# Block two of a two-block transformer layer on one core: where the head outputs are kept, gated and merged

## The chip, the cores and the metric

The kernel runs on one core of a Trainium2 chip. The metric is the device time of one execution in microseconds (us), the median of several runs. A profiled execution has its own time and its span, which runs from the first to the last instruction. Engines are named as in the profile: PE is TensorE (PEld its weight loads), ACT is ScalarE, DVE is VectorE, POOL is GpSimd, SP is SyncE; ACTq and SPq are the issues of DMAs by those engines.

## What is computed

The reference is two transformer blocks in a row on one sequence of 512 tokens by 1024 features, in float32. Block one (mLSTM heads, stick-breaking heads, an MLP) is untouched here. Block two, cut to what matters:

```python
h = rms_norm_2(x, norm_gain)
proj = h @ w_in                      # c_q, c_kv, ..., gate_a, gate_b, ..., m_a, m_b
# kind 0: 8 MLA heads of width 64 (causal softmax), kind 1: 8 DSA heads of width 64
#         (softmax over the top 128 keys that an indexer picks)
o_a = mla_attention(q_a, k_a, v_a) * silu(gate_a)        # 512 x 512
o_b = dsa_attention(q_b, k_b, v_b, ...) * silu(gate_b)   # 512 x 512
m = sigmoid([m_a, m_b] + b_merge)
y = m[0] * (o_a @ w_branch_mla) + m[1] * (o_b @ w_branch_dsa)
x = x + y @ w_out
```

`silu(g)` is `g * sigmoid(g)`, so an output is multiplied once by `g` and once by `sigmoid(g)`.

## The kernel before

Everything is one program with five instruction streams that meet at counting semaphores (`S[name]`). Activations stand transposed in SBUF, features on the 128 partitions and the 512 tokens along the free axis; `o_all[:, i]`, `g_all[:, i]` and `m_all[:, j]` are such tiles of 128x512. Weights come in groups `g` of 1024x512 from `wall`: SP loads a group in two halves into `w_raw`, ACT rounds a half to the short format (`split_hi`, L255), DVE makes the remainder (`split_lo`, L261). `project` (L288) then makes one 128x512 product tile in PSUM bank `proj[:, n % 2]` as three matmuls for each k tile (hi x hi, hi x lo, lo x hi). Before tile `n` PE waits for `tile_free >= n - 1`, so at most two tiles are unevicted; `tile_made` counts what PE made, `tile_free` what was evicted.

The end of block two has three stages.

1. **Head pairs B = 0 to 7** (0 to 3 are kind 0, 4 to 7 kind 1). In each pair PE does: turn q and k (L1379), gate tile 0, scores (L1386), gate tile 1, turn p (L1396), gate tile 2, p times v (L1404). The 24 gate tiles `T_L + 3 B + i` are `gate_a`, `gate_b` (8 tiles) and `m_a`, `m_b` (16 tiles); ACT evicts each to `gate_st` and stores it to DRAM (`gates_d`, L781 and L783). DVE does the masked maxima and the normalization, ACT the exponentials (L760), the eviction of p transposed (`head_pT`, L766) and of the pair's output (`head_out`, L773), which goes to `o_st` and from there to DRAM (`o_d`, L806). POOL stages q, k and v (L450, L451, L472). In loop form (`Fori`) two pairs are one iteration.
2. **Branch products, tiles T_BR + 0 to 15**, below T0 to T15: T0 to T7 multiply kind 0's gated outputs by `w_branch_mla` (group G_BR), T8 to T15 kind 1's by `w_branch_dsa` (G_BR + 1); a tile is 12 matmuls. PE's tile T0 waits for the four remainders of kind 0 (`oh_lo`), T8 for those of kind 1. DVE evicts each tile by multiplying it with its merge gate (L1208).
3. **Final product, T_FIN + 0 to 7**, 24 matmuls each, on the merged activations; DVE adds them to `x_fin` and SP stores the result.

Between stages 1 and 2 the outputs come back: POOL loads `o_all[:, 0:4]` and `g_all` in pair 5 (L481, L482), `o_all[:, 4:7]` and `m_all[:, 0:6]` after pair 7's staging (L489, L494), `o_all[:, 7:8]` when pair 7's output is stored (L496), then `m_all[:, 6:16]` (L499) and `x_fin` (L500). POOL multiplies `o_all` by `g_all` (L486 for tiles 0 to 3 in pair 6, L504 for 4 to 7). The function `gated(kind, ...)` stands in ACT's and in DVE's stream: ACT takes the sigmoid of `g_all` (L815), DVE multiplies (L1184), ACT rounds to `h_hi` (L818), DVE makes `h_lo` (L1190). In ACT's stream the order after pair 7 is `gated(0)`, sigmoids of merge gates 0 to 3 (`merge_gates`, L823), both halves of `split_hi(G_BR + 1)`, merge gates 4 and 5, `gated(1)`, merge gates 6 to 15. In DVE's stream it is `gated(0)`, then a loop over the 16 tiles, with `split_lo(G_BR + 1)` ahead of the evictions of T1 and T2 and kind 1's gating spread over T3 to T7; `split_lo(G_FIN)` stands ahead of T10 and T12. From T8 on POOL adds the two kinds (L508), ACT rounds the sum (`mg_hi`, L837) and DVE makes `mg_lo` (L1194).

## Time and profile before

| what | us |
|---|---|
| median of 3 runs | 1409.86 (1407.19 to 1410.21) |
| the profiled execution: its time | 1410.33 |
| the profiled execution: its span | 1408.6 |
| mean granted TensorE clock | 0.977 of full |
| PE busy / PEld busy | 1331.4 / 1066.5 |
| DVE / ACT / POOL busy | 701.6 / 638.7 / 124.8 |

What lies around the span of the profiled execution is 1.7 us. Engine times overlap, so they don't add up to the span; what sets the end is read from the chain of work that ended last, and what an engine's idle time is worth from the wait that ended it. Matmul records overlap their neighbours by some tenths of a microsecond, so the pace of PE is taken from start to start.

### The profile page before, as it was taken

Reading aid. Unit: us, or ns where it says so; the run is one execution under the profiler, and the core shown is the slowest. Engines: PE = TensorE matmul, PEld = TensorE weight load, DVE = VectorE, ACT = ScalarE, POOL = GpSimd, SP = SyncE. Lnnn points to the kernel's source line nnn. Section 1 sums busy time; section 2 is a strip of 40 time slices with the busy share of each in tenths; the row PEclk is TensorE's granted clock in tenths of the full one; section 3 lists DMA queues with packets and bytes.
Section 4 is the critical chain, followed back from the end, with each engine's and each line's share of the span. In section 5 each row is a group of like instructions: output and inputs, shape, how many; then the busy total and the mean of one; then the engine's idle time right before and its main releaser. Section 6 shows DMA issues by size and latency. Waiting matters only on the chain.

```text
span 1408.6 us, 16618 instructions
## 1 busy us (share of the span) xinstructions
PE 1331.4 (95%) x6008; PEld 1066.5 (76%) x6008; DVE 701.6 (50%) x1161; ACT 638.7 (45%) x927; POOL 124.8 (9%) x232
## 2 busy tenths in 40 slices
PE   4799999999999998999999999999878999999699
PEld 3677878777787776788888888878646777777577
DVE  5344443454444443452443424453798887443661
ACT  5455564555635561441332313353725454554540
POOL 1010100101000010000000000000112111140230
PEclk9899999999999999999999999999978999999899
DMA  5312122222222213123222322241111323535511
GB/s 204 105 64 89 53 89 76 84 67 67 97 67 93 67 63 140 69 94 116 89 89 92 111 95 89 94 170 69 60 60 55 118 97 102 205 102 188 209 60 60
DMA packets 26608, 138.05 MB, mean 98 GB/s; under 512 B 3400, under 2 KB 3464, under 8 KB 13520
## 3 DMA queue, kind: packets, MB, share of 16 engines
q1 hardware_dynamic: 15792, 109.06, 22.3%
q0 software_dynamic: 5168, 18.08, 3.9%
q10 hardware_dynamic: 5616, 10.49, 2.0%
q8 instruction: 19, 0.31, 0.1%
q14 instruction: 13, 0.11, 0.0%
HBM read 123.97 MB, written 12.60 MB: 97 GB/s over the span
## 4 chain that ended last, share of the span: by engine, by line
PE 89%; DVE 5%; ACT 3%; DMA 2%; issue 1%; ACTq 0%; POOL 0%; DVEq 0%; POOLq 0%
PE proj L288 72%; DMA x_res<-in_x 2%; PE pa L1288 2%; PE pm L1247 1%; PE pm L1295 1%; PE pm L1404 1%; PE pa L1254 1%; PE pa L1404 1%; PE pa L1247 1%; PE pa L1386 1%; PE pm L1386 1%; PE pa L1265 1%; PE pm L1396 1%; DVE rope L1034 1%; PE pm L1274 1%
## 5 line engine op out<-in xcount | busy, mean ns | idle before, releaser
L288 PE MATMUL proj<-h_hi,w_hi 128*128 128x512 f32 x1040 | 419.3, 403 | 17.7 <-DVE h_lo L1190 11.0
L288 PE MATMUL proj<-h_lo,w_hi 128*128 128x512 f32 x1040 | 407.7, 392 | 0.0
L288 PE MATMUL proj<-h_hi,w_lo 128*128 128x512 f32 x1040 | 407.6, 392 | 0.0
L261 DVE TENSOR_TENSOR w_lo<-w_raw,w_hi 128x2048 fp32r<-128x2048 f32 x102 | 234.3, 2309 | 172.6 <-ACT w_hi L255 170.0
L255 ACT ACTIVATE w_hi<-w_raw 128x2048 fp32r<-128x2048 f32 x102 | 193.4, 1911 | 159.0 <-PE proj L288 147.1
L288 PEld LDWEIGHTS proj<-h_hi,w_hi 128*128 128x128 f32 x1040 | 197.1, 189 | 65.2 <-issue 18.2
L288 PEld LDWEIGHTS proj<-h_hi,w_lo 128*128 128x128 f32 x1040 | 196.8, 189 | 42.3
L288 PEld LDWEIGHTS proj<-h_lo,w_hi 128*128 128x128 f32 x1040 | 197.3, 190 | 41.5 <-issue 2.9
L288 PE MATMUL proj<-w_hi,act_hi 128*128 128x512 f32 x256 | 99.6, 389 | 0.0
L288 PE MATMUL proj<-w_hi,act_lo 128*128 128x512 f32 x256 | 99.6, 389 | 0.0
L288 PE MATMUL proj<-w_lo,act_hi 128*128 128x512 f32 x256 | 99.6, 389 | 0.0
L999 DVE TENSOR_TENSOR x_res<-x_res,proj 128x512 f32<-128x512 f32 x32 | 21.9, 686 | 101.8 <-PE proj L288 101.8
L641 ACT ACTIVATE relu<-proj 128x512 f32<-128x512 f32 x32 | 19.2, 599 | 106.9 <-PE proj L288 106.9
L985 DVE TENSOR_TENSOR relu_sq<-relu 128x512 f32<-128x512 f32 x32 | 22.2, 694 | 76.3 <-ACT relu L641 76.3
L288 PEld LDWEIGHTS proj<-w_hi,act_hi 128*128 128x128 f32 x256 | 48.0, 188 | 10.1
L288 PEld LDWEIGHTS proj<-w_hi,act_lo 128*128 128x128 f32 x256 | 48.0, 188 | 10.0
L288 PEld LDWEIGHTS proj<-w_lo,act_hi 128*128 128x128 f32 x256 | 48.0, 188 | 9.9
L760 ACT ACTIVATE p_sb<-p_sb,mx 128x128 f32<-128x128 f32 (+1 forms) x64 | 35.1, 550 | 32.9 <-DVE mx L1133 32.9
L288 PE MATMUL proj<-w_hi,h_hi 128*128 128x512 f32 x96 | 38.0, 396 | 0.9 <-DVE h_lo L323 0.9
L288 PE MATMUL proj<-w_lo,h_hi 128*128 128x512 f32 x96 | 37.4, 390 | 0.0
L288 PE MATMUL proj<-w_hi,h_lo 128*128 128x512 f32 x96 | 37.4, 389 | 0.0
L422 POOL DMA_DIRECT2D x<-x_res x1 | 0.8, 769 | 402.1 <-DVE x_res L999 402.1
(354 smaller groups left out, 1865.3 us busy)
## 6 DMA issues: line engine op xcount, KB each, us to landing
w_raw<-in_wall SPq DMA_DIRECT2D x102, 1024.0 KB, 5.1
gates<-gate_st ACTq DMA_DIRECT2D x24, 256.0 KB, 2.0
m_all<-gates POOLq DMA_DIRECT2D x1, 2560.0 KB, 12.2
x_res<-in_x ACTq DMA_DIRECT2D x4, 512.0 KB, 11.7
bc<-gate_rows POOLq DMA_DIRECT2D x8, 256.0 KB, 3.4
x_res<-in_x POOLq DMA_DIRECT2D x1, 2048.0 KB, 11.7
x<-x_res POOLq DMA_DIRECT2D x1, 2048.0 KB, 7.1
heads_out<-o_st ACTq DMA_DIRECT2D x8, 256.0 KB, 2.0
```

The costliest lines, as they stand in the source:

```text
L255: nc.scalar.activation(w_hi[:, slot, 4 * half:4 * half + 4, :], w_raw[:, half], ACT.Copy)\
L261: nc.vector.tensor_tensor(w_lo[:, slot, 4 * half:4 * half + 4, :], w_raw[:, half], w_hi[:, slot, 4 * half:4 * half + 4, :], ALU.subtract)\
L288: mm = nc.tensor.matmul(proj[:, bank, :], lhsT, rhs, start=(k == 0 and q == 0), stop=(k == kts - 1 and q == 2))
L641: a.activation(relu[:, i % 2], proj[:, i % 2], ACT.Relu).then_inc(S["tile_free"], 1)
L760: a.activation(x, x, ACT.Exp, bias=mx[:, u, i:i + 1], accum_out=row_sum[:, u, i:i + 1])\
L985: v.tensor_tensor(relu_sq[:, i % 2], relu[:, i % 2], relu[:, i % 2], ALU.mult).then_inc(S["a_sq"], 1)
L999: v.tensor_tensor(xx, xx, proj[:, t % 2], ALU.add).then_inc(S["tile_free"], 1)
L1034: v.tensor_tensor(dst, xx, w, ALU.mult).then_inc(S["rope"], 1)
L1247: mm = t_.matmul(out_[:, TRI[i]:TRI[i] + SEQ - P * i], lhsT[0:rows, P * i:P * (i + 1)], rhs[0:rows, P * i:], start=True, stop=True)
L1288: mm = t_.matmul(pa[:, TRI[i] + P * (i2 - i):TRI[i] + SEQ - P * i], w[:, :], s_[:, TRI[i2]:TRI[i2] + SEQ - P * i2], start=(q == 0), stop=( ...
L1386: mm = t_.matmul(X[:, LOW[i]:LOW[i] + P * (i + 1)], qT[u][0:d, P * i:P * (i + 1)], kT[u][0:d, 0:P * (i + 1)], start=True, stop=True)
L1404: mm = t_.matmul(X[:, P * i:SEQ], v_st[u][:, i, :], pT[u][:, TRI[i]:TRI[i] + SEQ - P * i], start=(i == 0), stop=(i == TB - 1))
```

## The change

- `head_out` of pairs 4 to 7 writes straight into `o_all[:, B]` instead of `o_st`; the DRAM stores of these pairs and POOL's two loads of them (L489, L496) are gone. ACT's and DVE's loops over pairs 4 to 7 are written out.
- POOL loads `o_all[:, 0:4]` and `g_all` in pair 4 instead of pair 5. `m_all[:, 0:6]` waits for fewer gate stores, and the last load of merge gates is cut in two: `m_all[:, 6:10]` and `m_all[:, 10:16]`, after all gate stores and `pv0`; `x_fin` follows `o_sb1`.
- All eight products by `g_all` are on DVE (`times_g`): tiles 0 to 3 in pair 6, 4 to 7 after pair 7's DVE work. The eight merge sums are on DVE, right behind the eviction of T8 to T15.
- Kind 0's gating moves ahead of T0: in pair 7 ACT does the four sigmoids between gate tile 1 and `head_pT`, and the four roundings between `head_pT` and gate tile 2; DVE does the four products, `times_g(4)` to `times_g(6)`, and the four remainders.
- Rounded outputs stand in `og_hi` (over `g_all`) and `og_lo` (over `o_all`); the merged ones in `h_hi` and `h_lo`.
- ACT's order after pair 7 is: merge gates 0, 1; sigmoids of `g_all` 4 to 7; merge gates 2, 3; `split_hi(G_BR + 1)` twice; roundings 4 to 7; merge gates 4 to 15. DVE's: ahead of T1's eviction `split_lo` half 0 and products 4, 5; ahead of T2's `split_lo` half 1 and products 6, 7; remainders 4 to 7 ahead of T3 to T6.

```diff
@@ GpSimd
-                    if B == 5:
+                    if B == 4:
                         gp.wait_ge(S["o_stored"], 16 * 5)
-                        gp.wait_ge(S["gates_stored0"], 16 * 7)
-                        gp.wait_ge(S["gates_stored1"], 16 * 7)
+                        gp.wait_ge(S["gates_stored0"], 16 * 5)
+                        gp.wait_ge(S["gates_stored1"], 16 * 5)
...
                         gp.dma_start(o_all[:, 0:4], o_d[0:4].rearrange("k p n -> p k n")).then_inc(S["o_landed"], 16)
                         gp.dma_start(g_all[:, :, :], gates_d[0:KT].rearrange("k p n -> p k n")).then_inc(S["o_landed"], 16)
-                    if B == 6:
-                        gp.wait_ge(S["o_landed"], 32)
-                        for i in range(4):
-                            gp.tensor_tensor(o_all[:, i], o_all[:, i], g_all[:, i], ALU.mult).then_inc(S["o_times_g"], 1)
-
-            gp.wait_ge(S["o_stored"], 16 * 8)
-            gp.dma_start(o_all[:, 4:7], o_d[4:7].rearrange("k p n -> p k n")).then_inc(S["o_landed1"], 16)
+
             gp.wait_ge(S["v_staged0"], 16)
             gp.wait_ge(S["v_staged1"], 16)
-            gp.wait_ge(S["gates_stored0"], 16 * 10)
-            gp.wait_ge(S["gates_stored1"], 16 * 10)
+            gp.wait_ge(S["gates_stored0"], 16 * 8)
+            gp.wait_ge(S["gates_stored1"], 16 * 8)
             gp.dma_start(m_all[:, 0:6], gates_d[KT:KT + 6].rearrange("k p n -> p k n")).then_inc(S["m_landed0"], 16)
-            gp.wait_ge(S["o_stored"], 16 * 9)
-            gp.dma_start(o_all[:, 7:8], o_d[7:8].rearrange("k p n -> p k n")).then_inc(S["o_landed2"], 16)
             gp.wait_ge(S["gates_stored0"], 16 * 13)
             gp.wait_ge(S["gates_stored1"], 16 * 13)
-            gp.dma_start(m_all[:, 6:16], gates_d[KT + 6:3 * KT].rearrange("k p n -> p k n")).then_inc(S["m_landed1"], 16)
+            gp.wait_ge(S["pv0"], 8)
+            gp.dma_start(m_all[:, 6:10], gates_d[KT + 6:KT + 10].rearrange("k p n -> p k n")).then_inc(S["m_landed1"], 16)
+            gp.dma_start(m_all[:, 10:16], gates_d[KT + 10:3 * KT].rearrange("k p n -> p k n")).then_inc(S["m_landed2"], 16)
+            gp.wait_ge(S["o_sb1"], 9)
             gp.dma_start(x_fin[:, :, :], x2_d.rearrange("(t p) d -> p t d", p=P)).then_inc(S["x2_landed"], 16)
...
@@ ScalarE: pairs 4 to 7 and what follows them
+            for B in range(4, 8):
+                c, s = B // 2, B % 2
...
+                split_hi(G_L + B + 1, s, 1, used=T_L + 3 * B)
+                gate(c, s, 1)
+                if B == 7:
+                    for i in range(4):
+                        gate_sigmoid(i)
+                head_pT(0, B)
+                head_pT(1, B)
+                if B == 7:
+                    for i in range(4):
+                        gated_hi(i)
+                gate(c, s, 2)
+                head_out(0, B, o_all[:, B])
+                head_out(1, B, o_all[:, B])
...
-            gated(0, range(5))
-            merge_gates(range(4))
+            merge_gates((0, 1))
+            for i in range(4, 8):
+                gate_sigmoid(i)
+            merge_gates((2, 3))
             for hf in (0, 1):
                 split_hi(G_BR + 1, 0, hf, used=T_BR)
-            merge_gates((4, 5))
-            gated(1, range(5))
-            merge_gates(range(6, 2 * KT))
+            for i in range(4, 8):
+                gated_hi(i)
+            merge_gates(range(4, 2 * KT))
...
@@ VectorE
+            for B in range(4, 8):
...
+                split_lo(G_L + B + 1, B % 2, 1)
+                if B == 6:
+                    v.wait_ge(S["o_landed"], 32)
+                    for i in range(4):
+                        times_g(i)
+            for i in range(4):
+                gated(i)
+            for i in range(4, 7):
+                v.wait_ge(S["o_sb0"], i + 2)
+                v.wait_ge(S["o_sb1"], i + 2)
+                times_g(i)
+            for i in range(4):
+                low(i)
+            v.wait_ge(S["o_sb0"], 9)
+            v.wait_ge(S["o_sb1"], 9)
+            times_g(7)
...
-            gated(0, range(5))
             for j in range(2 * KT):
                 n = T_BR + j
-                if 3 <= j <= 7:
-                    gated(1, (j - 3,))
                 if j in (1, 2):
                     split_lo(G_BR + 1, 0, j - 1)
+                    gated(2 * j + 2)
+                    gated(2 * j + 3)
+                if 3 <= j <= 6:
+                    low(j + 1)
                 if j in (10, 12):
                     split_lo(G_FIN, 1, (j - 10) // 2)
...
                 v.tensor_tensor(m_all[:, j], proj[:, j % 2], m_all[:, j], ALU.mult).then_inc(S["tile_free"], 1)
+                if j >= KT:
+                    v.wait_ge(S["tile_free"], n + 1)
+                    v.tensor_tensor(m_all[:, j], m_all[:, j], m_all[:, j - KT], ALU.add).then_inc(S["merged"], 1)
                 if j > KT:
                     merged_low(j - KT - 1)
```

## Rows read from the trace of the kernel before

**Rows 1.** Page, part 1: busy time, share of span and instructions, engine by engine.
```profile
PE 1331.4 (95%) x6008; PEld 1066.5 (76%) x6008; DVE 701.6 (50%) x1161; ACT 638.7 (45%) x927; POOL 124.8 (9%) x232
```

**Rows 2.** Chain that ended last: start us, us, what; from pair 7's output on.
```profile
1304.40 0.60 ACT o_st L773
1305.21 0.34 ACTq L806
1305.78 1.28 ACT L815
...
1309.13 6.14 DVE h_lo L1190
...
1315.40 40.15 PE proj L288 x168
...
1356.14 49.27 PE proj L288 x216
```

**Rows 3.** Timeline of PE: start us, us, instruction, tile, idle before it.
```profile
1299.89 2.32 PE L1404 MATMUL pa<-pT,v_st 128*128 128x512 f32 x8
1302.04 2.32 PE L1404 MATMUL pm<-pT,v_st 128*128 128x512 f32 x8
...
1315.40 0.77 PE L288 MATMUL proj<-h_hi,w_hi 128*128 128x512 f32 x1 [11.04 <-DVE h_lo L1190]
...
1319.76 0.39 PE L288 MATMUL proj<-h_hi,w_hi 128*128 128x512 f32 x1
...
...
1361.71 0.39 PE L288 MATMUL proj<-w_hi,mg_hi 128*128 128x512 f32 x1
```

**Rows 4.** Half-microsecond windows of PE: us, PE busy (x), PEclk, DMA share, GB/s.
```profile
1308.00:1308.50 0.50, 0.00 (x0) 0.94 0.00 0
...
1407.00:1407.50 0.50, 0.00 (x0) 0.93 0.90 352
```

**Rows 5.** Timeline of ACT, from pair 7 to the second weight split.
```profile
1293.50 0.34 ACTq L783 DMA_DIRECT2D gates<-gate_st  x1
1293.89 1.24 ACT L766 ACTIVATE pT<-pa 128x1280 f32<-128x1280 f32 x1 [0.56 <-PE pa L1396]
...
1307.08 1.15 ACT L815 ACTIVATE g_all<-g_all 128x512 f32<-128x512 f32 x2
...
1317.63 2.55 ACT L823 ACTIVATE m_all<-m_all,merge_bias 128x512 f32<-128x512 f32 x4
1320.09 3.71 ACT L255 ACTIVATE w_hi<-w_raw 128x2048 fp32r<-128x2048 f32 x2
```

**Rows 6.** Timeline of DVE, pair 7 and the branch tiles.
```profile
1291.30 1.27 DVE L1141 TENSOR_SCALAR p_sb<-p_sb,row_sum 128x128 f32<-128x128 f32 x4
1292.89 2.29 DVE L261 TENSOR_TENSOR w_lo<-w_raw,w_hi 128x2048 fp32r<-128x2048 f32 x1 [0.32 <-ACT w_hi L255]
...
1320.02 0.69 DVE L1208 TENSOR_TENSOR m_all<-proj,m_all 128x512 f32<-128x512 f32 x1 [1.56 <-PE proj L288]
1322.09 2.29 DVE L261 TENSOR_TENSOR w_lo<-w_raw,w_hi 128x2048 fp32r<-128x2048 f32 x1 [1.39 <-ACT w_hi L255]
1324.30 0.68 DVE L1208 TENSOR_TENSOR m_all<-proj,m_all 128x512 f32<-128x512 f32 x1
1324.90 2.28 DVE L261 TENSOR_TENSOR w_lo<-w_raw,w_hi 128x2048 fp32r<-128x2048 f32 x1
...
1352.17 1.11 DVE L1194 TENSOR_TENSOR mg_lo<-m_all,mg_hi 128x512 fp32r<-128x512 f32 x1 [1.24 <-ACT mg_hi L837]
...
1355.41 0.68 DVE L1208 TENSOR_TENSOR m_all<-proj,m_all 128x512 f32<-128x512 f32 x1
```

**Rows 7.** Timeline of POOL: the products at the end of pair 7.
```profile
1309.78 4.92 POOL L504 TENSOR_TENSOR o_all<-o_all,g_all 128x512 f32<-128x512 f32 x4
```

**Rows 8.** DMA issues: out<-in, engine, op, count, KB each, median us to landing.
```profile
gates<-gate_st ACTq DMA_DIRECT2D x24, 256.0 KB, 2.0
m_all<-gates POOLq DMA_DIRECT2D x1, 2560.0 KB, 12.2
```

More of the change, by code:

```diff
@@ L808, in _ @@
-            a.wait_ge(S["tile_free"], T_BR)
-            def gated(kind, steps):
-                for i in steps:
-                    if i < 4:
-                        a.wait_ge(S["o_times_g"], 4 * kind + i + 1)
-                        a.activation(g_all[:, 4 * kind + i], g_all[:, 4 * kind + i], ACT.Sigmoid).then_inc(S["g_sig"], 1)
-                    if i >= 1:
-                        a.wait_ge(S["o_gated"], 4 * kind + i)
-                        a.activation(h_hi[:, 4 * kind + i - 1], o_all[:, 4 * kind + i - 1], ACT.Copy).then_inc(S["oh_hi"], 1)
+            with a.Fori(0, 2) as c:
+                for s in range(2):
+                    B = 2 * c + s
+                    split_hi(G_L + B + 1, s, 0, used=T_L + 3 * B)
+                    head_turns(0, B, QK_M)
+                    head_turns(1, B, QK_M)
+                    gate(c, s, 0)
+                    head_exp(0, B)
+                    head_exp(1, B)
+                    split_hi(G_L + B + 1, s, 1, used=T_L + 3 * B)
[3 more added lines that the diff above has]
+                    gate(c, s, 2)
+                    a.wait_ge(S["o_stored"], 16 * B + 16)
+                    head_out(0, B, o_st)
+                    head_out(1, B, o_st)
+                    a.wait_ge(S["o_sb0"], B + 2)
+                    a.wait_ge(S["o_sb1"], B + 2)
+                    a.dma_start(o_d[bass.ds(B, 1)].rearrange("a p n -> p (a n)"), o_st[:, :]).then_inc(S["o_stored"], 16)
@@ new lines, in _ @@
+            for B in range(4, 8):
+                c, s = B // 2, B % 2
+                split_hi(G_L + B + 1, s, 0, used=T_L + 3 * B)
+                head_turns(0, B, D_D)
+                head_turns(1, B, D_D)
+                gate(c, s, 0)
+                head_exp(0, B)
+                head_exp(1, B)
+                split_hi(G_L + B + 1, s, 1, used=T_L + 3 * B)
+                gate(c, s, 1)
+                if B == 7:
+                    for i in range(4):
+                        gate_sigmoid(i)
+                head_pT(0, B)
+                head_pT(1, B)
+                if B == 7:
+                    for i in range(4):
+                        gated_hi(i)
+                gate(c, s, 2)
+                head_out(0, B, o_all[:, B])
+                head_out(1, B, o_all[:, B])
@@ L1178, in gated @@
-            def gated(kind, steps):
-                for step in steps:
-                    i = 4 * kind + step
-                    if step < 4:
-                        v.wait_ge(S["g_sig"], i + 1)
-                        v.wait_ge(S["o_times_g"], i + 1)
-                        v.tensor_tensor(o_all[:, i], o_all[:, i], g_all[:, i], ALU.mult).then_inc(S["o_gated"], 1)
-                    if step:
-                        low(i - 1)
+            with v.Fori(0, 2) as b:
+                for s in range(2):
+                    B = 2 * b + s
+                    split_lo(G_L + B + 1, s, 0)
+                    for u in range(2):
+                        head_max(u, B, lambda i: causal[:, 384 - P * i:512], QK_M ** -0.5)
+                    head_norm(0, B)
+                    head_norm(1, B)
+                    split_lo(G_L + B + 1, s, 1)
+                    for rnd in range(4):
+                        top(B, rnd)
@@ new lines, in _, with times_g @@
+            v.wait_ge(S["top_out"], 49)
+            v.tensor_copy(idx[:, LOW[0]:LOW[0] + P], causal[:, 384:512]).then_inc(S["mask"], 1)
+            for i in range(1, TB):
+                x = idx[:, LOW[i]:LOW[i] + P * (i + 1)]
+                v.tensor_scalar(x, x, TAKEN / 2, NEG, ALU.is_gt, ALU.mult).then_inc(S["mask"], 1)
+            v.wait_ge(S["mask"], 4)
+            def times_g(i):
+                v.tensor_tensor(o_all[:, i], o_all[:, i], g_all[:, i], ALU.mult).then_inc(S["o_times_g"], 1)
```

90 lines of the change are left out of this document (26 added, 64 removed).

## The prediction, made before the changed kernel was run

> **What bounds the kernel now.** PE is busy for 95% of the span and the other engines for half of it or less [rows 1], so an edit outside PE's own work is worth only the PE idle time that it removes. The chain that ended last shows where such time is near the edit. After pair 7 it leaves PE and goes through ACT and DVE: output evicted at 1304.40, stored, a table load, sigmoid, product, rounding, a remainder of 6.14 us, and only then PE again, at 1315.40 [rows 2]. PE's timeline has this as 11.04 us idle in front of the branch tiles, released by the remainder L1190 [rows 3]. The 6.14 us belong to one 128x512 step on VectorE, of a size that takes 0.68 at 1324.30 [rows 6]; it began at 1309.13 and ended just after GpSimd's four products, 1309.78 to 1314.70 [rows 2, 7]. So four things lie in this gap: the store, the table load, kind 0's gating itself, and VectorE standing still beside GpSimd. Behind it PE is again the chain, with one hole before 1356.14, where 1315.40 plus 40.15 leaves 0.6 us [rows 2], after an eviction of T12 that ended at 1356.09; it stood behind a split, and that behind a remainder at 1352.17 that had waited 1.24 us for the rounding of GpSimd's sum and took 1.11 [rows 6].
>
> I use these paces. A branch tile is 12 matmuls at 49.27 / 216 = 0.228, so 2.72 us without the small loss at a start [rows 2]. PE can start T0 at 1302.04 + 2.16 = 1304.20, as pv of pm follows pv of pa after 2.15 [rows 3].
>
> **Part 1, kind 0's gating before T0.** It removes the gap if its last remainder is done by 1304.2. Follow ACT in pair 7 [rows 5]. It issues the store of gate tile 1 at 1293.50; a table load began 0.57 after such an issue (1305.21, 1305.78) and took 1.28 [rows 2], so the first sigmoid starts at 1295.4. Two sigmoids take 1.15, which is 0.54 from start to start [rows 5], so the fourth ends at 1297.6. The two evictions `head_pT` (1.24 each) follow: 1297.5 to 1298.7 and to 1299.9, where before the first started at 1293.89. PE wants the first at 1299.89 and the second at 1302.04 [rows 3]; that leaves 1.2 us and 2.1 us. VectorE ends `split_lo` at 1295.2 [rows 6], so its four products run behind the sigmoids, 0.60 apart (1324.30 to 1324.90 [rows 6]), and end at 1298.5; products by `g_all` of 4 to 6 end at 1300.3. ACT's four roundings run from 1299.8 to 1302.0, VectorE's remainders behind them to 1302.8. That is 1.4 us before 1304.2, so T0 doesn't wait. Gate tile 2, which PE ends at 1299.9, is evicted at 1302.0, and only T1 needs its bank, at 1306.9. `head_out` of pm still starts at 1304.40. Removed: 1315.40 - 1304.20 = 11.2 us.
>
> A ScalarE rule speaks against this place. The trace has 1.28 us for the load and the first sigmoid right behind it [rows 2]. The Trainium skill (ScalarE: Activation LUTs, "What ACT_TABLE_LOAD costs") gives about 1283 ns for the load and about 1380 ns more for a drain, 2.66 us in all. By that page the margin of 1.2 us at pv is used up and PE would lose about 0.2 us; by the row it loses nothing.
>
> **Part 2, the clock.** In the gap the granted clock fell: the window from 1308.00 shows 0.94, so it went from 2.4 to 1.2 GHz near its end, four us after PE's last matmul [rows 4]. T0 therefore took 1319.76 - 1315.40 = 4.36 us instead of 2.72 [rows 3]: 1.6 us more come back if the clock holds.
>
> **Part 3, what is late next.** T1 to T4 meet a VectorE that waits for ACT. After `head_out` (1304.40) ACT does two merge sigmoids, four sigmoids of `g_all` and two merge sigmoids before the split of G_BR + 1. A merge sigmoid is 0.61 from start to start (four from 1317.63 to 1320.09 [rows 5]). From 1304.94: 4 x 0.61 + 4 x 0.54 = 4.6, so the first split runs 1309.5 to 1311.4 and the second ends at 1313.3 (1.8 apart). VectorE's eviction of T0 (PE's next start + 0.26: 1319.76 to 1320.02 [rows 3, 6]) is done at 1308.0. For T1 it waits for the split: `split_lo` 1311.5, products 4 and 5 at 1313.7 and 1314.3 (2.21 and 0.60 later), eviction 1314.9 to 1315.6. T3 needs that bank. PE would reach T3 at 1304.2 + 3 x 2.72 + 0.1 = 1312.5 and starts it at 1315.7: **3.2 us idle**. T2's eviction stands behind the second split half and products 6 and 7: 1315.5 + 2.21 + 2 x 0.60 = 1318.9, to 1319.6. PE would reach T4 at 1318.5 and starts at 1319.7: **1.2 us idle**. From T5 (1322.5) VectorE has one remainder and one eviction, 1.3 us, per 2.72 us tile and catches up. ACT's roundings 4 to 7 end at 1319.6 and its merge sigmoids (0.61 each) stay ahead; T8 starts at 1330.7 and its remainders are ready by 1327. Before, PE did not wait here, since T0 itself was late: the split at 1320.09 met T0's end.
>
> **Part 4, the sums on VectorE.** The wait for GpSimd's sums and its slowing of VectorE (1.11 for 0.68 us) go, and with them the hole at 1356.14, 0.6 us [rows 2, 6]. Each tile from T8 on costs VectorE an eviction 0.69, a sum behind it (right behind the end of the eviction, not overlapping it as independent steps do, 0.60 apart) 0.70, and a remainder 0.60: 2.0 of 2.72 us. Two halves of `split_lo(G_FIN)`, ahead of T10 and T12, add 2 x 2.21. No row shows this sum on VectorE; the product of the same form took 0.68 and I take that. Run through, T10's eviction ends at 1341.2 against 1341.6 where T12 wants it, and T12's ends at 1347.2 against 1347.0: **0.25 us idle**. T15 ends at 1352.9, the last remainder is ready at about 1356 and T_FIN + 0 wants it 7 x 0.68 = 4.8 us after its start. The end of the branch stage is the eviction chain's, the rest PE's.
>
> **Part 5, loads.** The reloads of 3 MB move one pair earlier, into the same place of the pair; what they share the DMA engines with there is the same as before, a pair's weights and gate stores; I take nothing. `m_all[:, 0:6]` no longer waits for pair 6's store. The last loads need the store of gate tile 2, issued at 1302.7. A store of 256 KB lands 2.0 us later [rows 8], so they start at 1304.8. The old 2.5 MB load landed in 12.2 us [rows 8], so all merge gates are there by about 1318 and ACT asks for `m_all[:, 10]` at 1323.4. On POOL nothing is queued behind these issues. SP's own queue is not passed by anything. In pair 6 four products on VectorE (4 x 0.60 = 2.4 us) follow the pair's last split; ACT turns to the next pair only after the pair's output, which in pair 7 came 9 us behind that split (1295.2, 1304.40 [rows 2, 6]). So they cost nothing.
>
> **Sum.** Final product before: starts 1361.71 [rows 3]. After: 1304.2 + 16 x 2.72 (43.5) + 3.2 + 1.2 + 0.25 + 0.5 of start losses = 1352.9. Gain 8.8; from there on the work is the same. I take 0.3 off for a clock that falls in the new holes (next part): 8.5. The profiled execution took 1410.33, so 1401.8; the median of before lies 0.5 lower: **1401.3 us**.
>
> **Rivals.**
> A, the forecast: T3 and T4 wait for VectorE, 1401.3; own range 1400.0 to 1402.5.
> B, the clock falls and costs fully. For: at the end PE stopped at 1405.4 and the window from 1407.00 already shows the fall, two us later, less than the new hole of 3.2 [rows 2, 4]. Against: in the gap it held for four, and a slow T3 delays T4 to where its bank is free anyway, so 1.2 of 1.6 is absorbed. A fall in T4 or later isn't: 1401.0 + 1.6 = 1402.6.
> C, pair 7 is too full: evictions for pv or the remainders come late. Margins 1.2 and 1.4 us against a list of some sixteen instructions on two engines; if each handover costs 0.2 more, PE waits up to 2 us: 1403.3.
> D, VectorE bounds T8 to T15: 2.0 us plus splits leave 8 x 2.72 - 8 x 2.0 - 4.4 = 1.4 us in all. A sum of 1.0 instead of 0.7 brings 8 x 0.3 = 2.4, less what slack is left: 1402.3; at GpSimd's 1.26 (4.92 / 4, the outer bound [rows 7]) 4.5 less 1.4: 1404.4. Below nothing is excluded, since PE can't run ahead of its matmuls.
> E, the holes at T3 and T4 don't form: 8.8 + 4.4, so 1396.6. It needs ACT to reach the split 3 us sooner, which its order excludes.
> F, on the other side: the streams of ACT and DVE written out for pairs 4 to 7 starve while code is loaded. Place: between the exponentials and the turning of p; the normalization of pm ended at 1292.57, and PE turned pm once pa was turned, at most by 1293.89, when ACT evicted that [rows 5, 6], so about 1 us is spare. From there on every us late is PE's, four times. It decides from 3.2 us late per pair, as 4 x (3.2 - 1) = 8.8 eats the gain; at 4.2 us it gives 1401.3 + 12.8 = 1414.1. Nothing in the trace asks for that: one stream without loops serves the end of block two, with PE unbroken for 49 us [rows 2]. The Trainium skill (Runtime: NRT & Kernel Launch, "Instruction fetch mechanics") says that straight code is prefetched in order and that it is the taken branch that stalls; by that page F gives no loss. No run here shows it yet.
> That the change doesn't do what it says would mean T0 still waits near 1315: nothing it waits for is left there, so I give that no share of its own.
>
> **How the numbers follow.** A 0.52, B 0.15, C 0.12, D 0.13, E 0.03, F 0.03, the rest 0.02 nearly no change. The range 1399.5 to 1404.6 takes in A to D with their bounds and leaves out E, F and the rest. A measurement of this kernel tells about 0.2% (2.8 us) from no change. Faster by more, so under 1407.0: 0.95; within: 0.03, the rest and a third of F; slower: 0.02, what is left of F.
>
> **What would show it.** Right: T0's first matmul near 1304.2 with no idle time before it; PE idle before T3 (about 3 us) and T4 (about 1) put down to DVE L1208's eviction; the table load in pair 7 at 1294; evictions and remainders at 0.68 with no GpSimd beside them; the final product from about 1353. Wrong: idle PE before pv of pair 7 or before T0 (C), PE waits in T11 to T15 beyond 0.3 us (D), a clock of 1.2 GHz after 1308 (B), no PE idle at T3 (E), or PE waits at the turning of p in pairs 4 to 6 (F).

## The result, and the profile after

| what | before | after |
|---|---|---|
| median | 1409.03 (6 runs, 1407.19 to 1410.21) | 1398.45 (1397.07 to 1401.48) |
| ratio to before | 1 | 0.9929, 95% interval 0.9916 to 0.9942 |
| the profiled execution: time / span | 1410.33 / 1408.6 | 1397.07 / 1395.3 |
| mean granted TensorE clock | 0.977 | 0.983 |

One of the six executions of after took 3250.04 us: it is left out of the range and the ratio, but the median of 1398.45 counts it, and the other five have 1398.30.

The change is faster by 0.7%, about 10 us. The forecast was 1401.3 with a range of 1399.5 to 1404.6, so the direction was right, and the median lies 1.0 us below the range.

The page of after, its head and part 1 (before in [rows 1]):
```profile
span 1395.3 us, 16528 instructions
PE 1327.9 (95%) x6008; PEld 1064.2 (76%) x6008; DVE 704.7 (51%) x1177; ACT 638.1 (46%) x927; POOL 102.4 (7%) x215
```
PE does the same 6008 matmuls and is still busy for 95% of the span. POOL lost 22 us of work and DVE took on only 3: a step that moved costs DVE about half of what it cost POOL (0.68 against 1.26), and DVE steps that had been stretched in before, one of them to 6.14 us, are short again.

The chain that ended last in after (start us, us, what), which answers to [rows 2]:
```profile
1297.72 2.17 PE pm L1426 x8
...
1299.92 0.59 ACT o_all L759
...
1301.78 2.18 ACT g_all L763 x4
1303.96 1.23 ACT m_all L825 x2
1305.19 3.62 ACT w_hi L255 x2
...
1309.30 1.28 DVE o_all L1181 x2
1310.59 0.61 DVE m_all L1227
...
1311.24 2.74 PE proj L288 x11
1313.99 0.60 DVE o_all L1181
1314.59 0.61 DVE m_all L1227
...
1315.25 24.79 PE proj L288 x108
1340.04 2.21 DVE w_lo L261
1342.24 0.61 DVE m_all L1227
...
1342.90 49.27 PE proj L288 x216
```
The chain no longer holds PE up in front of T0. It leaves PE where it did before, behind pair 7's pv, but comes back only at T3: through ACT's list (two merge sigmoids, four sigmoids of `g_all`, two merge sigmoids, two weight splits), DVE's products and the eviction of T1. It holds PE up twice more, at T4 and at T14.

PE's timeline of after (start us, us, instruction, idle before it), which answers to [rows 3]: pair 7's two pv, then the first matmuls of T0, T3, T4, T14 and the final product.
```profile
1295.41 2.32 PE L1426 MATMUL pa<-pT,v_st 128*128 128x512 f32 x8
1297.56 2.32 PE L1426 MATMUL pm<-pT,v_st 128*128 128x512 f32 x8
1299.64 0.48 PE L288 MATMUL proj<-og_hi,w_hi 128*128 128x512 f32 x1
...
1311.24 0.50 PE L288 MATMUL proj<-og_hi,w_hi 128*128 128x512 f32 x1 [3.15 <-DVE m_all L1227]
...
1315.25 0.50 PE L288 MATMUL proj<-og_hi,w_hi 128*128 128x512 f32 x1 [0.99 <-DVE m_all L1227]
...
1342.90 0.50 PE L288 MATMUL proj<-og_hi,w_hi 128*128 128x512 f32 x1 [0.16 <-DVE m_all L1227]
...
1348.47 0.39 PE L288 MATMUL proj<-w_hi,h_hi 128*128 128x512 f32 x1
```
T0 follows pv with no idle time. The final product starts 53.06 us after pair 7's pv (1348.47 - 1295.41), where before took 1361.71 - 1299.89 = 61.82 [rows 3]: 8.76 us less. The rest of the difference lies elsewhere: pair 7's pv itself starts 4.48 us earlier in after's execution (1299.89 against 1295.41), in front of any code that the prediction gave a gain to. From the final product's start to the end of the execution both take the same, 1410.33 - 1361.71 = 48.62 and 1397.07 - 1348.47 = 48.60. So the 13.26 us between the two profiled executions are 8.76 in the stage that the change is about, 4.48 ahead of it and 0.02 behind.

### The profile page after: what moved, and what is told of

Read it like the earlier page. It is cut to its first block, busy times and chain, and to the rows that moved or that the text cites. A ratio compares the mean times of both kernels' runs of the same rounds, so it can differ in the third digit from the quotient of the medians.

```text
span 1395.3 us, 16528 instructions
## 1 busy us (share of the span) xinstructions
PE 1327.9 (95%) x6008; PEld 1064.2 (76%) x6008; DVE 704.7 (51%) x1177; ACT 638.1 (46%) x927; POOL 102.4 (7%) x215
## 4 chain that ended last, share of the span: by engine, by line
PE 88%; DVE 5%; ACT 3%; DMA 2%; issue 1%; POOL 0%; ACTq 0%; DVEq 0%; POOLq 0%
PE proj L288 72%; DMA x_res<-in_x 2%; PE pa L1310 2%; PE pm L1269 1%; PE pm L1317 1%; PE pm L1426 1%; PE pa L1276 1%; PE pa L1426 1%; PE pa L1269 1%; PE pa L1408 1%; PE pm L1408 1%; PE pa L1287 1%; DVE rope L1038 1%; ACT w_hi L255 1%; PE pm L1418 1%
## 5 line engine op out<-in xcount | busy, mean ns | idle before, releaser
L288 PE MATMUL proj<-h_hi,w_hi 128*128 128x512 f32 x976 | 393.0, 403 | 5.5 <-DVE h_lo L323 5.5
L288 PE MATMUL proj<-h_hi,w_lo 128*128 128x512 f32 x976 | 382.0, 391 | 0.0
L288 PE MATMUL proj<-h_lo,w_hi 128*128 128x512 f32 x976 | 381.8, 391 | 0.0
L288 PEld LDWEIGHTS proj<-h_hi,w_hi 128*128 128x128 f32 x976 | 184.6, 189 | 48.8 <-issue 7.0
L288 PEld LDWEIGHTS proj<-h_lo,w_hi 128*128 128x128 f32 x976 | 184.6, 189 | 39.1 <-issue 2.9
L288 PEld LDWEIGHTS proj<-h_hi,w_lo 128*128 128x128 f32 x976 | 184.2, 189 | 39.4
L288 PE MATMUL proj<-w_hi,h_hi 128*128 128x512 f32 x160 | 63.6, 397 | 0.9 <-DVE h_lo L323 0.9
L288 PE MATMUL proj<-w_hi,h_lo 128*128 128x512 f32 x160 | 63.0, 394 | 0.0
L288 PE MATMUL proj<-w_lo,h_hi 128*128 128x512 f32 x160 | 62.9, 393 | 0.0
L288 PEld LDWEIGHTS proj<-w_hi,h_hi 128*128 128x128 f32 x160 | 30.4, 190 | 9.3 <-issue 2.6
## 6 DMA issues: line engine op xcount, KB each, us to landing
x_res<-in_x POOLq DMA_DIRECT2D x1, 2048.0 KB, 11.8
```

The lines of the kernel that those rows point to most:

```text
L288: mm = nc.tensor.matmul(proj[:, bank, :], lhsT, rhs, start=(k == 0 and q == 0), stop=(k == kts - 1 and q == 2))
```

## The experiments

The theory: the change is worth the stage from pair 7's pv to the final product, 8.8 us, and the 4.5 us ahead of it are a scatter of the executions. The rival for the 4.5 us: the edits in pairs 4 to 7 (written-out loops, direct output, earlier loads) made the upstream part faster. The times that the experiments turn on stand in one table. T_FIN is the start of the final product. A ratio is to the runs of the kernel before on the same chip (medians 1407.96 to 1409.03), and the last five columns are starts in PE's timeline in each kernel's profiled execution, and the time from pair 7's pv to T_FIN, below "the stage":

| kernel | median us (ratio to before, 95%) | pair 0's pv | pair 7's pv | T0 | T_FIN | pair 7's pv to T_FIN |
|---|---|---|---|---|---|---|
| before | 1409.03 | 1094.90 | 1299.89 | 1315.40 | 1361.71 | 61.82 |
| after | 1398.45 (0.9916 to 0.9942) | 1090.42 | 1295.41 | 1299.64 | 1348.47 | 53.06 |
| c_before | 1407.62 (0.9986 to 1.0005) | 1091.18 | 1296.18 | 1311.69 | 1358.92 | 62.74 |
| c_after | 1398.82 (0.9915 to 0.9942) | 1091.08 | 1296.06 | 1300.29 | 1349.12 | 53.06 |
| e_unroll | 1408.81 (0.9989 to 1.0007) | 1094.76 | 1299.75 | 1315.11 | 1361.49 | 61.74 |
| e_split_first | 1397.59 (0.9898 to 0.9925) | 1094.58 | 1299.57 | 1303.80 | 1349.39 | 49.82 |
| e_spread | 1393.61 (0.9882 to 0.9915) | 1091.18 | 1296.19 | 1300.42 | 1344.31 | 48.12 |
| e_late | 1405.02 (0.9969 to 0.9989) | 1092.55 | 1297.54 | 1309.67 | 1357.15 | 59.61 |
| e_products | 1403.55 (0.9950 to 0.9979) | 1094.23 | 1299.22 | 1309.30 | 1356.50 | 57.28 |
| e_pool_sums | 1400.33 (0.9926 to 0.9959) | 1091.45 | 1296.45 | 1300.68 | 1350.17 | 53.72 |
| e_fill | 1402.20 (0.9936 to 0.9969) | 1094.19 | 1301.65 | 1305.99 | 1355.23 | 53.58 |
| e_sum_twice | 1402.26 (0.9936 to 0.9969) | 1092.89 | 1297.88 | 1302.11 | 1353.05 | 55.17 |

**Both kernels again, c_before and c_after**, without an edit.

> The kernel before, not edited, timed against itself. Theory one: the ratio is 1.000 within 0.001, single executions differ by 2 to 4 us, and the profile reaches the first pv of pair 0 at another time than 1094.9, between 1090 and 1096. Rival (early gain due to the edit): it comes at 1094.9 within 0.5 again.

> The changed kernel once more, not edited. In the profiled executions the changed kernel reached the first pv of pair 0 4.5 us sooner than the one before, in code that neither edit touches, and then gained 8.8 us in the branch stage. Theory one (the granted clock of TensorE in the stages up to pair 0 differs from execution to execution and nothing else): in a new profile the time to that pv (1094.9 in before, 1090.4 in after) moves by some us, the span follows it, and the branch stage from T0 to T_FIN + 0 stays at 48.6 us within 0.3. The median of this kernel minus that of before is then 8.8 us plus or minus 1. Rival (the edit itself speeds up the early stages): the early 4.5 us stand in every execution, and the difference of the medians is 11 to 13 us.

Measured: the kernel before once more shows pair 0's pv at 1091.18, 3.72 us earlier than in its first trace, and the kernel after at 1091.08. So the same program differs by 3.72 of the 4.48 us. Where the two traces of before part can be read off PE's timelines: 0.51 us by the start of block one's heads, 0.33 more by block two's norm, 1.30 more by the turning of `t_k` and 1.58 more up to pair 0's pv. The two largest are clock levels. The turning of pair 0's second p, in the first trace of before (PE's timeline, idle before it in brackets):
```profile
1086.72 2.39 PE L1396 MATMUL pm<-ident,p_sb 128*128 128x128 f32 x10 [1.11 <-DVE p_sb L1141]
```
and in c_before:
```profile
1084.54 1.31 PE L1396 MATMUL pm<-ident,p_sb 128*128 128x128 f32 x10 [1.11 <-DVE p_sb L1141]
```
The windows of the same place (stretch, us, busy us and count of PE, PEld, DVE, ACT, POOL, then PEclk, DMA share, GB/s), in before:
```profile
996.00:1012.00 16.00, 11.68 (x42) 8.87 (x43) 8.91 (x8) 12.77 (x23) 0.00 (x0) 0.89 0.35 121
1086.00:1088.00 2.00, 1.28 (x6) 1.28 (x7) 1.94 (x3) 1.43 (x3) 1.03 (x2) 0.64 0.00 0
```
and in c_before:
```profile
996.00:1012.00 16.00, 12.54 (x54) 9.48 (x55) 10.94 (x10) 13.40 (x24) 0.65 (x1) 1.00 0.40 133
1086.00:1088.00 2.00, 2.00 (x10) 1.62 (x9) 2.00 (x5) 1.94 (x2) 1.81 (x2) 1.00 0.35 131
```
In one execution the clock fell to 1.2 GHz at two places where in the other it stayed at 2.4 GHz: near 998 behind an idle time of 2.42 us in both, and at 1086 after idle times of 2.68 and 1.11 us in the one and 2.52 and 1.11 in the other. Each such fall costs about 1.5 us (1.30 and 1.58 here), as T0 did in [rows 3]. The slow turning of p (2.1 to 2.4 us) stands in the traces of before, e_unroll, e_products, e_split_first, e_late, e_sum_twice and e_fill, the quick one (1.3 to 1.7) in c_before, after, c_after, e_spread and e_pool_sums. (In e_spread and e_pool_sums the first p was turned slowly, 2.40 us, without making pv late.) The fall near 998 stands in before, e_unroll, e_products, e_split_first and e_fill. With both falls pair 0's pv starts at 1094.2 to 1094.9, with the one at 1086 alone at 1092.6 and 1092.9, with neither at 1090.4 to 1091.5. Each group with both or neither holds kernels with the old and with the new end of block two, so the rival falls.

The times of whole executions show it too. Of the 21 executions of before measured beside c_before, ten took 1406.65 to 1407.76, ten 1409.45 to 1410.21, and one 1408.34, which is the median. The profiled executions with both falls in this kernel and in e_unroll took 1410.33 and 1410.10, the one with neither 1407.53. A median of a few executions lands in one group or the other: the 1409.86 that the prediction started from came out of three and lay 1.5 us above the median of 21.

The stage itself repeats: 53.06 in both traces of after. Before it is 61.82 and 62.74, and 61.74 in e_unroll. The idle time ahead of T0 is the same 11.0 us, but in c_before T0 to T_FIN took 47.23 against 46.31, as the low clock lasted longer. So the gain of the stage is 8.8 to 9.7 us.

**The loops written out, e_unroll**, on the kernel before: ACT's and DVE's streams for pairs 4 to 7.
```diff
-                with a.Fori(0, 2) as b:
-                    for s in range(2):
+            with a.Fori(0, 2) as b:
+                for s in range(2):
+                    act_pair(0, QK_M, b, s)
+            for b in range(2):
+                for s in range(2):
+                    act_pair(1, D_D, b, s)
```


> The kernel before with one part of the change: ACT's and DVE's loops over pairs 4 to 7 are written out. Theory one: nothing on PE's path depends on it, ratio 1.000 within 0.001 and pairs 4 to 7 take 29.5 us each on PE as before. Rival (the code's form matters): if the early 4.5 us come from the form of the code, this kernel shows them too, ratio 0.997; if written out streams starve, PE waits at the turning of p and the ratio is over 1.002.

Measured: no difference (0.9989 to 1.0007), and from pair 0's pv to pair 7's 204.99 us, with loops in before 204.99, in after 204.99. Rival F falls: the written-out streams don't starve. The sentence of the Trainium skill that the prediction cited (Runtime: NRT & Kernel Launch, "Instruction fetch mechanics": straight code is prefetched in order, and a taken branch stalls when its target lies outside the pages that are held) agrees with this as far as straight code goes; no run here shows a stall at a taken branch that PE would have felt.

**Kind 0's gating back behind pair 7, e_late**, on after; all else stays.
```diff
-                if B == 7:
-                    for i in range(4):
-                        gate_sigmoid(i)
                 head_pT(0, B)
                 head_pT(1, B)
-                if B == 7:
-                    for i in range(4):
-                        gated_hi(i)
...
+            for i in range(4):
+                gate_sigmoid(i)
+            for i in range(4):
+                gated_hi(i)
             merge_gates((0, 1))
```


> The changed kernel with one part undone: kind 0's four sigmoids and four roundings stand behind pair 7's output again instead of inside pair 7. On-chip outputs and VectorE's sums and products stay. Theory: PE is idle for 7.3 us before T0 (1.3 table load, sigmoids, products, roundings and remainders one behind the other), the clock falls (1.6), the hole at T3 (3.3) is absorbed and that at T4 stays: from pair 7's first pv to T_FIN + 0 takes 58.8 us instead of 53.1, median near 1404.5. Rival: if the place in pair 7 is not what counts but VectorE's freedom from GpSimd and the stores that are gone, PE is idle for under 4 us and the loss is under 3 us.

PE's timeline of e_late (as above):
```profile
1309.67 0.76 PE L288 MATMUL proj<-og_hi,w_hi 128*128 128x512 f32 x1 [7.65 <-DVE og_lo L1183]
```
ACT's timeline of e_late, right behind pair 7's last output:
```profile
1302.66 1.28 ACT L763 ACT_TABLE_LOAD   x1
1303.96 2.19 ACT L763 ACTIVATE g_all<-g_all 128x512 f32<-128x512 f32 x4
1306.05 2.17 ACT L767 ACTIVATE og_hi<-o_all 128x512 fp32r<-128x512 f32 x4
```
Measured: 59.61 us for the stage, 6.55 more than after, and 6.2 more in the median than c_after's 1398.82. PE waits 7.65 us for table load, sigmoids and roundings in a row, its clock is low again when T0 starts (0.76 against 0.48 for the first matmul), and the hole at T3 goes, since T3 now comes late anyway; the one at T4 stays (1.0 us). So with the rest of the change in place, the gating's place in pair 7 is worth 6.6 us of the stage.

**Only the products of tiles 4 to 7 on VectorE, e_products**, on the kernel before: they leave GpSimd's stream and stand in VectorE's behind `gated(0)`.
```diff
             for i in range(4, 8):
                 if i in (4, 7):
-                    gp.wait_ge(S["o_landed1" if i == 4 else "o_landed2"], 16)
-                gp.tensor_tensor(o_all[:, i], o_all[:, i], g_all[:, i], ALU.mult).then_inc(S["o_times_g"], 1)
+                    v.wait_ge(S["o_landed1" if i == 4 else "o_landed2"], 16)
+                v.tensor_tensor(o_all[:, i], o_all[:, i], g_all[:, i], ALU.mult).then_inc(S["o_times_g"], 1)
```


> The kernel before with one part of the change: products 4 to 7 are on VectorE, behind kind 0's gating, instead of on GpSimd beside it. Theory: the remainder of 6.13 us was VectorE standing still beside GpSimd and takes 0.68, T0 starts 5.5 us sooner, and about 0.5 of it is lost again at T3; median 5.0 us under that of before, ratio 0.9965. Rival: the 6.13 us are waiting for a load or for ACT, the remainder stays at several us and the ratio is 0.999 or more.

PE's timeline of e_products:
```profile
1309.30 0.77 PE L288 MATMUL proj<-h_hi,w_hi 128*128 128x512 f32 x1 [5.60 <-DVE h_lo L1185]
```
DVE's timeline of e_products, the first remainder of kind 0:
```profile
1308.46 0.69 DVE L1185 TENSOR_TENSOR h_lo<-o_all,h_hi 128x512 fp32r<-128x512 f32 x1
```
Measured: the remainder that took 6.14 us in [rows 2] takes 0.69, PE's idle time falls from 11.04 to 5.60, and the median by 4.4 us (1407.96 to 1403.55). Half of the gap was one VectorE step stretched beside GpSimd's products; the loads stayed where they were, so they weren't its cause. Moving four products alone brings almost half of the change's gain. Its 4.5 us of the stage and e_late's 6.6 don't add up to the change's 8.8, since both shorten the same wait.

**The sums back on GpSimd, e_pool_sums**, on after.
```diff
+            for i in range(KT):
+                gp.wait_ge(S["tile_free"], T_BR + KT + i + 1)
+                gp.tensor_tensor(m_all[:, KT + i], m_all[:, KT + i], m_all[:, i], ALU.add).then_inc(S["merged"], 1)
...
-                if j >= KT:
-                    v.wait_ge(S["tile_free"], n + 1)
-                    v.tensor_tensor(m_all[:, j], m_all[:, j], m_all[:, j - KT], ALU.add).then_inc(S["merged"], 1)
```


> The changed kernel with the eight sums back on GpSimd. Theory: the sums are hidden on either engine up to T11; on GpSimd VectorE's remainders and split halves beside them take 1.1 and up to 3.4 us and wait for the rounding, and a hole of 0.8 us before T14 or T15 comes back: 0.5 to 1.5 us slower than the changed kernel from T0 to T_FIN + 0 (48.8). Rival: the sums on VectorE were themselves what costs there; then this kernel is faster than the changed one.

DVE's timeline of e_pool_sums:
```profile
1334.20 3.38 DVE L261 TENSOR_TENSOR w_lo<-w_raw,w_hi 128x2048 fp32r<-128x2048 f32 x1
...
1340.63 1.10 DVE L1215 TENSOR_TENSOR h_lo<-m_all,h_hi 128x512 fp32r<-128x512 f32 x1 [1.25 <-ACT h_hi L844]
```
POOL's timeline of the same stretch:
```profile
1333.77 1.67 POOL L498 TENSOR_TENSOR m_all<-m_all 128x512 f32<-128x512 f32 x1 [1.43 <-DVE m_all L1230]
```
Measured: the stage takes 53.72, 0.66 more than after, with a hole of 0.62 us at T14 in place of 0.16. Beside a GpSimd sum a weight split takes 3.38 us instead of 2.29 and a remainder 1.10 instead of 0.68; an eviction beside one, which reads a PSUM bank, kept its 0.68 (at 1338.71, with GpSimd busy from 1338.27 to 1341.19). The intervals of the two kernels overlap, so the trace decides here and not the medians.

**What pair 7 still holds, e_fill**, on after: six more sigmoids on ACT ahead of `head_pT`, one behind the other, into a buffer that `head_pT` overwrites.
```diff
+                    for i in range(6):
+                        a.activation(pT[1][:, 0:512], causal[:, :], ACT.Sigmoid).then_inc(S["fill"], 1)
+                        a.wait_ge(S["fill"], i + 1)
                 head_pT(0, B)
```


> The changed kernel with six more sigmoids of 128x512, one waiting for the other, on ACT in pair 7, right behind the four of kind 0 (0.62 us each and about 0.06 from end to start, 4.1 us in all). They add work and leave none out. Theory: ACT's block in pair 7 is free only as far as its margin. In the changed kernel the first p was evicted at 1293.87 and PE took it at 1295.41, so 1.5 us are spare: PE now waits 4.1 - 1.5 = 2.6 us before the first pv, and no longer before the second pv or T0; the median is 2.6 us above the changed kernel's, 1401.3. Rival (later margins are smaller: the remainders of kind 0, ended 1.6 us before T0): PE waits at T0 too and the loss is 4 us or more.

PE's timeline of e_fill:
```profile
1301.65 2.42 PE L1429 MATMUL pa<-pT,v_st 128*128 128x512 f32 x8 [2.35 <-ACT pT L753]
```
ACT's timeline of e_fill:
```profile
1296.39 3.94 ACT L814 ACTIVATE pT<-causal 128x512 f32<-128x512 f32 x6
1300.36 1.24 ACT L753 ACTIVATE pT<-pa 128x1280 f32<-128x1280 f32 x1
```
Measured: 3.94 us of extra work make PE wait 2.35 us ahead of pv, so the margin is about 1.6 us; the stage behind takes 53.58 against 53.06, and 0.36 of that stands already in the eviction of T4, behind a fall of the clock at T3 (see e_sum_twice). The extra work is PE's once the margin is used up, which is what rival C needed.

**A second sum, e_sum_twice**, on after: one more 128x512 step on VectorE with each of the eight sums, into a place that is written again.
```diff
                     v.wait_ge(S["tile_free"], n + 1)
+                    v.tensor_tensor(h_lo[:, j - KT], m_all[:, j], m_all[:, j - KT], ALU.add)
                     v.tensor_tensor(m_all[:, j], m_all[:, j], m_all[:, j - KT], ALU.add).then_inc(S["merged"], 1)
```


> The changed kernel with one more VectorE step of 128x512 for each of T8 to T15, the sum computed a second time into a buffer that the remainder then overwrites. Theory: in the changed kernel VectorE is within 0.65 us of bounding T12 and already bounds T14 (a hole of 0.3 us), so 0.60 us more per tile comes through from T12 on: T10 and T11 wait at most 0.1 us, T14 waits 1.8 us more, and T0 to T_FIN + 0 takes 50.6 us instead of 48.8. Rival (VectorE has the 1.4 us of slack that the sum of its work against PE's showed, before T14 as after it): 3 of 4.8 us come through and spread over T12 to T15, 52 us; or, if PE's queue hides them, less than 0.5.

DVE's timeline of e_sum_twice:
```profile
1339.45 0.69 DVE L1227 TENSOR_TENSOR m_all<-proj,m_all 128x512 f32<-128x512 f32 x1
1340.17 0.69 DVE L1230 TENSOR_TENSOR h_lo<-m_all 128x512 fp32r<-128x512 f32 x1
...
1341.98 0.68 DVE L1227 TENSOR_TENSOR m_all<-proj,m_all 128x512 f32<-128x512 f32 x1
```
PE's timeline of e_sum_twice, and a window of the place (columns as above):
```profile
1313.72 0.79 PE L288 MATMUL proj<-og_hi,w_hi 128*128 128x512 f32 x1 [3.15 <-DVE m_all L1227]
```
```profile
1313.50:1314.00 0.50, 0.28 (x1) 0.28 (x2) 0.50 (x2) 0.23 (x1) 0.00 (x0) 0.63 1.05 434
```
Measured: T0 to T_FIN takes 50.94 where after takes 48.83, 2.1 us more. Not all of it is the sums: the hole at T3 is the same 3.15 us as in after, but here the clock had fallen to 1.2 GHz at its end, T3 ran slowly, the hole at T4 vanished into it, and T4's eviction started 19.00 us after T0 instead of 18.72. So the fall costs 0.3 us and the eight steps of 0.60 cost 1.8, as expected. From one eviction to the next it is 2.53 us of a tile's 2.72, so the two splits are what no longer fits. VectorE is close to its bound in T10 to T14 in after, and over it only at T14, by 0.16.

**The holes at T3 and T4, e_split_first and e_spread.** First ACT's weight splits ahead of its other work:
```diff
             merge_gates((0, 1))
+            for hf in (0, 1):
+                split_hi(G_BR + 1, 0, hf, used=T_BR)
             for i in range(4, 8):
                 gate_sigmoid(i)
             merge_gates((2, 3))
-            for hf in (0, 1):
-                split_hi(G_BR + 1, 0, hf, used=T_BR)
```


> The changed kernel with ACT's two halves of the split of G_BR + 1 moved ahead of the sigmoids of g_all 4 to 7 and merge gates 2 and 3. Theory: the idle time of PE before T3 (3.1 us) and T4 (1.0 us) comes from VectorE waiting for this split. Worked out with the rows of the changed kernel: T3 doesn't wait, T4 waits 1.0 us, so 3.1 us less than the changed kernel. Rival: T3 waits for the products by sigmoid that stand ahead of T1's eviction, or for the loads; then 1 us or less is gained.

PE's waits in e_split_first (waiting for: us in total, times, longest us); in after the same line is `4.3, 3, 3.1`:
```profile
PE proj L288 <- DVE m_all L1227: 1.1, 2, 1.0
```
Measured: the stage takes 49.82, 3.24 less; the hole at T3 is gone and the one at T4 stays. The median fell by only 1.2 against c_after. Its profiled execution is one with both falls of the clock and reached pair 0's pv at 1094.58, 3.5 us later than c_after's. With five executions of a kernel that scatters by some 4 us, the 3 us are seen in full in the stage; that the scatter hides the rest in the median is likely, and not shown.

Then also DVE's products and remainders for kind 1 behind the evictions of T3 to T6 instead of ahead of T1 to T6, each half of `split_lo(G_FIN)` right behind an eviction (T9, T11) and ahead of that tile's sum, and, in ACT's stream, merge gates 4 to 6 ahead of the roundings (not in the cut):
```diff
                 if j in (1, 2):
                     split_lo(G_BR + 1, 0, j - 1)
-                    gated(2 * j + 2)
-                    gated(2 * j + 3)
-                if 3 <= j <= 6:
-                    low(j + 1)
-                if j in (10, 12):
-                    split_lo(G_FIN, 1, (j - 10) // 2)
...
                 v.tensor_tensor(m_all[:, j], proj[:, j % 2], m_all[:, j], ALU.mult).then_inc(S["tile_free"], 1)
+                if j in (3, 4):
+                    gated(2 * j - 2)
+                    gated(2 * j - 1)
+                if j in (5, 6):
+                    low(2 * j - 6)
+                    low(2 * j - 5)
+                if j in (9, 11):
+                    split_lo(G_FIN, 1, (j - 9) // 2)
```


> The changed kernel with ACT's split of G_BR + 1 first, and VectorE's stream spread: T1 and T2 are evicted right behind the split halves, products 4 to 7 follow the evictions of T3 and T4, remainders 4 to 7 those of T5 and T6, and the halves of the split of G_FIN stand behind the evictions of T9 and T11. Theory: PE has no idle time in the branch stage, so T0 to T_FIN + 0 takes 44.4 us (48.8 in the changed kernel, 45.6 with only the split moved), and the median is 4.4 us under the changed kernel's, near 1394.4. Rival (the loads of the merge gates or VectorE's work per tile are late next): some of the 1.2 us beyond the moved split stays, 45.0 us or more.

DVE's timeline of e_spread, from T0's eviction:
```profile
1303.53 0.69 DVE L1221 TENSOR_TENSOR m_all<-proj,m_all 128x512 f32<-128x512 f32 x1 [1.44 <-PE proj L288]
...
1306.77 0.68 DVE L1221 TENSOR_TENSOR m_all<-proj,m_all 128x512 f32<-128x512 f32 x1
```
Measured: the stage takes 48.12, 4.94 less than after, with no wait of PE from T0 on; T1's eviction starts 6.35 us after T0's first matmul, where in after it is 10.87 (1310.51 - 1299.64). The median is 1393.61, 14.35 under that of before, where the stage is 13.7 to 14.6 us shorter. Its interval (0.9882 to 0.9915) ends where those of after and c_after begin (0.9916 and 0.9915), and its slowest execution (1396.24) was quicker than the quickest of after (1397.07): this version is faster than both kernels.

## Why the prediction was right or wrong

**The stage was right in its terms.** Placed on the same time axis, 4.48 us later, after's starts fall on the working:

| step of the prediction | predicted | measured (+ 4.48) |
|---|---|---|
| T0 | 1304.2, no wait | 1304.12, no wait |
| first p eviction done, margin to pv | 1.2 | 1.5 |
| last remainder of kind 0, margin to T0 | 1.4 | 1.6 |
| T3 starts; idle | 1315.7; 3.2 | 1315.72; 3.15 |
| T4 starts; idle | 1319.7; 1.2 | 1319.73; 0.99 |
| idle at T14 | 0.25 | 0.16 |
| final product | 1352.9 | 1352.95 |

Part 1 rests on pair 7's list in ACT and DVE. ACT's timeline in after:
```profile
1289.25 1.28 ACT L763 ACT_TABLE_LOAD   x1 [0.40 <-ACT gate_st L775]
1290.54 2.20 ACT L763 ACTIVATE g_all<-g_all 128x512 f32<-128x512 f32 x4
1292.65 1.22 ACT L753 ACTIVATE pT<-pa 128x1280 f32<-128x1280 f32 x1
...
1294.88 2.17 ACT L767 ACTIVATE og_hi<-o_all 128x512 fp32r<-128x512 f32 x4
```
DVE's timeline in after:
```profile
1295.54 2.50 DVE L1185 TENSOR_TENSOR og_lo<-o_all,og_hi 128x512 fp32r<-128x512 f32 x4
1300.62 0.69 DVE L1177 TENSOR_TENSOR o_all<-o_all,g_all 128x512 f32<-128x512 f32 x1 [2.58 <-ACT o_all L759]
```
The first p eviction ends at 1293.87 and PE wants it at 1295.41; the remainders end at 1298.04 and T0 starts at 1299.64. The table load began 0.37 us after the gate store's issue, not 0.57 as assumed from the issue at the end of pair 7, which is most of the difference. The page cited against this place (the Trainium skill, ScalarE: Activation LUTs, "What ACT_TABLE_LOAD costs") gives about 1.38 us for a drain on top of the load: the trace doesn't agree, since ACT is idle for 0.40 us ahead of the load and not at all behind it (1289.25 + 1.28 is 1290.53, and the sigmoid starts at 1290.54). With the measured margin of 1.5 us it would not have cost PE anything either way.

**Part 2 had the right mechanism, and a size that was too small by up to 0.9.** 1.6 us for the low clock in T0 was that one execution's; in c_before it was 2.5.

**Part 3 was right, and the 0.3 taken off for the clock was not needed in these executions.** The middle of both new holes, PE's windows in after (columns as above):
```profile
1309.50:1310.00 0.50, 0.00 (x0) 0.00 (x0) 0.50 (x2) 0.00 (x0) 0.00 (x0) 1.00 1.02 418
1314.50:1315.00 0.50, 0.00 (x0) 0.00 (x0) 0.50 (x2) 0.50 (x2) 0.00 (x0) 1.00 1.09 459
```
The clock held at 2.4 GHz through 3.15 us, here and in c_after, so rival B did not come in the changed kernel's traces. That was partly luck: behind the same tiles it fell at the end of the same 3.15 us in e_sum_twice, and in e_fill, where the hole is 3.23 us, just after T3 had begun. It then cost 0.3 to 0.4 us, since most of it went into the hole at T4, as B's working says (0.4).

**Part 4 was right.** The sum took 0.69 us where 0.68 was assumed (DVE's timeline of after):
```profile
1329.24 0.69 DVE L1227 TENSOR_TENSOR m_all<-proj,m_all 128x512 f32<-128x512 f32 x1 [2.03 <-PE proj L288]
1329.96 0.69 DVE L1230 TENSOR_TENSOR m_all<-m_all 128x512 f32<-128x512 f32 x1
```
Rival D's outer bound, GpSimd's 1.26, was far off. Its way of counting, 1.4 us of slack over all tiles and every further microsecond PE's, prices such work too high: eight steps of 0.60 more, 4.8 us, would cost 3.4 by it and cost 1.8 in e_sum_twice. **Part 5 was right**: from pair 0's pv to pair 7's nothing moved by a hundredth.

**What failed is the base of the sum.** The prediction took its gain from "the profiled execution took 1410.33", moved by 0.5 to the median of three, 1409.86. Both came from the upper of the two groups that the times of this kernel form; the median of 21 executions is 1408.34, 1.5 us lower. Ahead of the change the profiled execution had two falls of the clock that c_before didn't have. Two smaller terms went the same way: the 0.3 taken off for the clock, and up to 0.9 in part 2. With a base of 1408.34 and the stage's 8.8 to 9.7 us the sum is 1398.7 to 1399.6; measured were 1398.45 and 1398.82. The work behind the stage was taken as fixed in so many words ("from there on the work is the same") and the work ahead of it silently, while the runs shown, 1407.19 to 1410.21, already said that one kernel scatters by 3 us. The range was built from the costs of the edit alone: its low end of 1399.5 lay 1.8 us under A's sum, and had no term for the base. A term of 1.5 us to either side would have held the time.

The account is good to about a microsecond, and no better. Against the six executions of before that stand beside it (1409.03), after gained 10.6 us, about 1 to 2 us more than the stage; the interval of the ratio, 8.2 to 11.8 us, has room for both. Whether the clock falls less often in the changed kernel's first 1090 us is not shown.

Of the rivals, C and D have the right mechanisms (e_fill, e_sum_twice), but C's margins were not used up and D's wait stayed at 0.16 us; E could not happen in the change's own order, as the prediction said, but its size was right: 4.4 us by its working for the two holes, and 4.94 in e_spread, which also takes away the wait at T14 and some start losses, by another order on ACT and DVE. F did not happen.

What is left open: what decides whether the clock falls at 1086, near 998 or at T3 in a given execution, and what the outputs kept on chip are worth by themselves. No run here tells.

## What to carry to other kernels

When a stall is taken out, follow both engines' lists to the next place where PE needs a buffer: here a third of what was removed came back as smaller holes (4.3 of some 13 us), and the next edit (here the weight split ahead of the gating and the evictions ahead of both) is read from the same list. A step on GpSimd is priced by what it does to the VectorE steps beside it too, not by its own time alone: four products cost PE 5.4 us of waiting at T0, though PE needed their results only for T8. And a prediction in microseconds needs a term for its base: look first whether the times of one kernel form groups, compare the same stage in two traces for the effect of the edit, and take the scatter of the untouched part from the runs.
